# First mixing reordered on three engines, gate products cut into 64x64 halves

## The reference

```
u = rmsnorm(h, g_pre_mix)
q, k, v, xr, yr = split(u @ w_in)                    # 512, 128, 128, 512, 512 columns
s = q k^T / 8 within a window of 128; p = exp(s - m) / (sum(exp(s - m)) + exp(sink - m))
attn = p @ v                                          # 8 heads of 64, two blocks of queries
xr = causal_conv(xr, 4 taps) + conv_b
gate_r, gate_i = xr @ w_a, xr @ w_x                   # 8 diagonal blocks of 64x64 each
r, i = sigmoid(gate_r + b_a), sigmoid(gate_i + b_x)
a = exp(-8 r softplus(-lam)); hr = scan(a, sqrt(1 - a^2) * (i * xr))
rec = gelu(yr) * hr
h = h + rmsnorm(concat(attn, rec) @ w_out, g_post_mix)
```

## Time and profile before

| | us |
|---|---|
| median of 3 runs | 888.44 |
| lowest, highest | 888.41, 888.63 |
| the profiled execution | 888.37 |
| its span | 886.6 |
| PE busy in the span | 874.9 |
| DVE busy | 585.6 |
| ACT busy | 525.3 |
| POOL busy | 24.6 |

### The profile page before, as it was taken

One profiled execution on the slowest core, in us unless ns is written; L12 is line 12 of the kernel. 1 busy time (PEld: TensorE's weight loads), 2 busy tenths in 40 slices (PEclk: granted clock), 3 DMA queues, 4 the chain that ended last, 5 costly groups with the idle time before them and its releaser, 6 DMA issues.

```text
span 886.6 us, 17878 instructions
## 1 busy us (share of the span) xinstructions
PE 874.9 (99%) x7067; PEld 811.9 (92%) x7067; DVE 585.6 (66%) x950; ACT 525.3 (59%) x927; POOL 24.6 (3%) x36
## 2 busy tenths in 40 slices
PE   9999999999999999999999999999999999999997
PEld 6988899999998999999999999999988999999986
DVE  4689865555556666668787878556767555554576
ACT  6478664444446765665968676765558444444463
POOL 4100300000000000000000000000000000000000
PEclk9999999999999999999999999999999999999999
DMA  9913775555554464545324142335565565565541
GB/s 282 271 65 112 199 199 190 188 188 188 189 189 143 143 190 143 161 151 163 125 67 144 50 143 77 116 122 170 185 201 191 190 189 189 189 189 189 183 150 48
DMA packets 107655, 143.24 MB, mean 162 GB/s; under 512 B 3032, under 2 KB 95448, under 8 KB 107600
## 3 DMA queue, kind: packets, MB, share of 16 engines
q1 hardware_dynamic: 105648, 137.60, 48.4%
q0 software_dynamic: 1744, 4.67, 2.4%
q10 hardware_dynamic: 208, 0.20, 0.1%
HBM read 141.41 MB, written 1.05 MB: 161 GB/s over the span
## 4 chain that ended last, share of the span: by engine, by line
PE 90%; DVE 5%; ACT 4%; issue 1%; DMA 0%; DVEq 0%; ACTq 0%
PE ps L1853 17%; PE ps L1855 16%; PE ps L1854 16%; PE ps L1859 9%; PE ps L1861 9%; PE ps L1860 9%; PE ps L2237 2%; PE ps L2224 1%; PE ps L2245 1%; ACT wh L640 1%; PE ps L1951 1%; PE ps L2212 1%; DVE wl L1214 1%; DVE R L1250 0%; PE ps L1932 0%
## 5 line engine op out<-in xcount | busy, mean ns | idle before, releaser
L1214 DVE TENSOR_TENSOR wl<-w_raw,wh 128x1024 fp32r<-128x1024 f32 x251 | 304.7, 1223 | 216.2 <-ACT wh L640 215.6
L1853 PE MATMUL ps<-xTh,wh 128*128 128x256 f32 (+1 forms) x1160 | 331.2, 286 | 1.3 <-DVE xTl L1240 0.8
L1855 PE MATMUL ps<-xTh,wl 128*128 128x256 f32 (+1 forms) x1160 | 326.3, 281 | 0.0
L1854 PE MATMUL ps<-xTl,wh 128*128 128x256 f32 (+1 forms) x1160 | 326.3, 281 | 0.0
L640 ACT ACTIVATE wh<-w_raw 128x1024 fp32r<-128x1024 f32 x251 | 263.6, 1055 | 80.0 <-PE ps L1861 58.9
L1853 PEld LDWEIGHTS ps<-xTh,wh 128*128 128x128 f32 x1160 | 219.0, 189 | 5.3 <-issue 3.2
L1854 PEld LDWEIGHTS ps<-xTl,wh 128*128 128x128 f32 x1160 | 218.3, 188 | 1.9 <-issue 1.0
L1855 PEld LDWEIGHTS ps<-xTh,wl 128*128 128x128 f32 x1160 | 219.3, 189 | 0.0
L1859 PE MATMUL ps<-wh,y 128*128 128x512 f32 x224 | 87.9, 392 | 0.0
L1861 PE MATMUL ps<-wh,y 128*128 128x512 f32 x224 | 87.6, 391 | 0.0
L1860 PE MATMUL ps<-wl,y 128*128 128x512 f32 x224 | 87.1, 389 | 0.0
(11 more groups left out here) (390 smaller groups left out, 1265.3 us busy)
## 6 DMA issues: line engine op xcount, KB each, us to landing
w_raw<-in_w_in_dram SPq DMA_DIRECT2D x42, 1024.0 KB, 5.2
w_raw<-in_w_ff_dram SPq DMA_DIRECT2D x32, 1024.0 KB, 5.3
w_raw<-in_w_ffn_gate_dram SPq DMA_DIRECT2D x11, 1024.0 KB, 5.4
w_raw<-in_w_ffn_up_dram SPq DMA_DIRECT2D x11, 1024.0 KB, 5.3
w_raw<-in_w_ffn_down_dram SPq DMA_DIRECT2D x11, 1024.0 KB, 5.0
w_raw<-in_w_out_dram SPq DMA_DIRECT2D x8, 1024.0 KB, 4.9
w_raw<-in_w_proj_a_dram SPq DMA_DIRECT2D x4, 1024.0 KB, 5.4
w_raw<-in_w_proj_b_dram SPq DMA_DIRECT2D x4, 1024.0 KB, 5.3
```

What stands on the lines that cost most here:

```text
L1214: TT(low_part, raw_unit(SLOT[p], j, layout), high_part.bitcast(F32), ALU.subtract).then_inc(w_lo, 1)
L1853: mm(out, wh_, xh, start=first, stop=False)
L1854: mm(out, wh_, xl, start=False, stop=False)
L1855: return mm(out, wl_, xh, start=False, stop=last)
```

## The change

Four edits, all in the first mixing.

1. On DVE, `soft_sums(1)` goes ahead of `lo(13)`, `lo(14)` ahead of the combination that frees the square root, the scans ahead of what were `lo(16)` and `lo(17)`; these two low parts leave DVE.
2. They go to GpSimd, as one `tensor_tensor` each, which waits for the high part and for all low parts in front of it. DVE's `lo(18)` waits for both.
3. On PE, two weight steps of `rec_unit(0)` go ahead of `scores(0)`, one of `rec_unit(2)` ahead of `scores(1)`, three of `gelu_unit(1)` ahead of `p_transposes(0)`.
4. Each gate product of 128x128 becomes two of 64x64, one for each diagonal block, on the upper and the lower half of the partitions.

```
@@ gpsimd
             pool.dma_start(cst[:, C_COS:C_END], A["cst"][:, C_COS:C_END]).then_inc(cst_loaded, 16)
 
+            for n in (16, 17):
+                pool.wait_ge(w_hi, n + 1)
+                pool.wait_ge(w_lo, n)
+                high_part, low_part = unit_parts(n, "rows")
+                pool.tensor_tensor(low_part, raw_unit(SLOT[n // 2], n % 2, "rows"), high_part.bitcast(F32), ALU.subtract).then_inc(w_lo, 1)
+
             pool.wait_ge(gain_used, 1)
@@ vector
             convolve(1)
             lo(12)
+            soft_sums(1)
             lo(13)
-            soft_sums(1)
 
             dve.wait_ge(i_act, LT)
...
             link(TT(a2, a_, a_, ALU.mult))
+            lo(14)
             dve.wait_ge(a_tanh_out, 2 * LT)
             STT(th_, a2, 1.0, th_, ALU.add, ALU.mult).then_inc(m2_out, 1)
             oT_lo(0)
-            lo(14)
             lo(15)
             dve.wait_ge(mult_out, 1)
             link(TT(xc, a2, xc, ALU.mult))
             oT_lo(1)
-            lo(16)
             for m in range(LT):
                 ins = dve.tensor_tensor_scan(r_g[:, m, :], a_[:, m, :], xc[:, m, :], 0.0, ALU.mult, ALU.add)
             link(ins)
-            lo(17)
             dve.wait_ge(gelu_out, 1)
             TT(gy, gy, r_g[:, :, META:T1], ALU.mult).then_inc(rec_out, 1)
+            dve.wait_ge(w_lo, 18)
             lo(18)
@@ tensor
+            def some(steps, n):
+                for _ in range(n):
+                    next(steps)
+
+            steps = rec_unit(0)
+            some(steps, 2)
             for b in range(2):
                 pe.wait_ge(emptied[b], EMPTIED[6][b])
             scores(0)
-            rec_unit(0)
-            rec_unit(1)
+            run(steps)
+            run(rec_unit(1))
+            steps = rec_unit(2)
+            some(steps, 1)
             scores(1)
-            rec_unit(2)
-            rec_unit(3)
-            gelu_unit(0)
+            run(steps)
+            run(rec_unit(3))
+            run(gelu_unit(0))
+            steps = gelu_unit(1)
+            some(steps, 3)
             p_transposes(0)
-            gelu_unit(1)
+            run(steps)
...
-                mm(fm[:, m % 2, 0:T1], wa_bd[:, m, :], xc[:, m, :], start=True, stop=True)
-                mm(acc[:, m, 0:T1], wx_bd[:, m, :], xc[:, m, :], start=True, stop=True).then_inc(r_ps, 1)
+                for bd, out in ((wa_bd, fm[:, m % 2, 0:T1]), (wx_bd, acc[:, m, 0:T1])):
+                    for half in (slice(0, 64), slice(64, P)):
+                        last = mm(out[half], bd[half, m, half], xc[half, m, :], start=True, stop=True)
+                last.then_inc(r_ps, 1)
```

More of the change, by code:

```diff
@@ L2047, in rec_unit @@
             def rec_unit(m):
-                run(fm_steps(6 + m, xTh, xTl, 0, T1))
+                return fm_steps(6 + m, xTh, xTl, 0, T1)
             def gelu_unit(m):
-                run(fm_steps(10 + m, xTh, xTl, META, S))
+                return fm_steps(10 + m, xTh, xTl, META, S)
+            def some(steps, n):
[3 more added lines that the diff above has]
+            some(steps, 2)
             for b in range(2):
@@ L2070, in _ @@
                 pe.wait_ge(emptied[m % 2], EMPTIED[GATE_UNIT][m % 2] - LT // 2 + m // 2)
-                mm(fm[:, m % 2, 0:T1], wa_bd[:, m, :], xc[:, m, :], start=True, stop=True)
-                mm(acc[:, m, 0:T1], wx_bd[:, m, :], xc[:, m, :], start=True, stop=True).then_inc(r_ps, 1)
+                for bd, out in ((wa_bd, fm[:, m % 2, 0:T1]), (wx_bd, acc[:, m, 0:T1])):
+                    for half in (slice(0, 64), slice(64, P)):
+                        last = mm(out[half], bd[half, m, half], xc[half, m, :], start=True, stop=True)
+                last.then_inc(r_ps, 1)
             p_transposes(1)
[L2074 to L2077, removed]
+            run(gelu_unit(2))
+            steps = gelu_unit(3)
+            some(steps, 2)
             outputs(1)
```

## The result

The changed kernel takes 890.25 us (median of 20 runs, 888.69 to 890.66), the kernel before, timed beside it, 888.74 (20 runs, 888.22 to 889.31). The ratio is 1.0017, its 95% interval 1.0011 to 1.0023: slower by 1.0 to 2.0 us, and the time lies above the forecast range, which ended at 889.4.

The account below looks back on a forecast made before the run. PE was taken as the bound, busy 874.9 of 886.6 us, with 1.76 us of waits as ceiling; 888.37 - 0.63 - 0.25 + 1.08 + 0 gave 888.57, with 0.07 for the median 888.6; range 887.2 to 889.4.

Parts of the forecast that it names:

- Weight steps: On PE: steps ahead of the scores bring later ones 0.63 us earlier; three ahead of the first transposes delay these 0.26.
- The two steps ahead of `scores(0)`: On PE: six products run inside the 0.72 us wait, so all weight steps behind the scores come 0.63 us earlier.
- DVE's chain to the second transposes: From DVE's copy to the softmax sums, ending at 68.10: PE starts the second transposes at 68.20, gaining 0.88 us.
- Gate halves: Gate products on PE: the two 64x64 halves run side by side, 0 us.
- POOL: Low parts on GpSimd: 2.35 us each; lo(16) holds DVE's root product until 79.45, +1.08 us.
- The step from no hindrance to the held product: At the output projection's second tokens: the delayed root product adds 1.08 us, PE starting at 81.52 instead of 80.44.
- No hindrance: Rival, DVE's root product beside POOL: hindered for less than the 0.4 us margin, 887.6, up to 887.9; chance 0.33.
- DVE first: Rival, DVE's root product beside POOL: DVE always goes first, POOL works in its pauses, 888.9 us; chance 0.10.
- Serial gates: Rival, gate products on PE: halves run one after the other, +2.5 us, 890.9; chance 0.05.
- The case of all waits gone: Rival, PE in the first mixing: all three waits vanish, -1.76 us, 886.7; chance 0.03.
- the middle case: The forecast, DVE's root product: the later instruction waits for the earlier, PE's second tokens 0.20 us later, 888.6; chance 0.45.
- something not thought of: Anywhere: a remainder for causes the prediction did not list, no size given; chance 0.04.

Follow-up runs that it names:

- a4: The kernel before with the gate halves alone, no other edit: 888.34 us, ratio 1.0002 to the kernel before.
- a2: The changed kernel with the low parts of units 16 and 17 back on DVE, nothing on POOL: 888.98 us, ratio 1.0005 to the kernel before.
- b1: The kernel before with only the low parts of units 16 and 17 moved from DVE to GpSimd: 889.72 us, ratio 1.0014.
- m2: The changed kernel without the three gelu_unit(1) steps ahead, low parts back on DVE, plus idle GpSimd fills: 887.87 us, ratio 0.9993 to the kernel before.
- a1: The changed kernel with the three weight steps of gelu_unit(1) back behind the first transposes: 888.67 us, ratio 1.0004 to the kernel before.
- m1: The changed kernel without the three gelu_unit(1) steps ahead, low parts back on DVE, plus idle two-input GpSimd products: 891.26 us, ratio 1.0031.
- g3: The changed kernel with lo(11) moved ahead of soft_sums(0) on DVE, GpSimd's low parts kept: 889.02 us, ratio 1.0007 to the kernel before.

## Why the prediction was wrong

**Weight steps: the step that failed.** "The three steps ahead of the first transposes (nine products, 1.1 us) move these from ... 56.56 to about 57.65, that is 0.26 later than before." The nine products were taken as ready to run. They need `lo(11)`, which DVE's list has behind the first softmax product: before, that product runs from 55.89 to 57.25, and the low part behind it until 57.17 + 1.22 = 58.39. The timeline of DVE before:

```profile
57.17 1.22 DVE L1214 TENSOR_TENSOR wl<-w_raw,wh 128x1024 fp32r<-128x1024 f32 x1
```

At their old place, from 59.06, the products found it done. In the changed kernel PE therefore stood 1.25 us in front of them, and the first transposes came 1.63 late, not 0.26. The softmax that they were to cover had long ended: in the changed kernel it was done at 57.06, PE could start at 58.25. Everything needed was in the trace of before; what the moved products wait for at their new place was not asked. The two steps ahead of `scores(0)` did what was said (PE at 56.72 is 0.62 ahead, 0.63 forecast).

**DVE's chain to the second transposes** was right in its links: the copy of the transposed block started 2.01 us later than before on the clock, 1.63 counted from the last query product, one low part (1.13) is saved, and 0.50 is left. Forecast with the 0.26, it was -0.88. The difference of 1.38 is the error at the first transposes, nothing else. The idle time left there, 1.04, is the 1.0 of the forecast.

**Gate halves**: 0, right; a4 shows it alone.

**POOL**: right in kind and size. Shifted by 0.38 for the later start and by 1.38 for the failed step, the forecast has POOL's piece from 78.83 (79.00 in the trace), the product's end at 82.52 (82.56) and the second tokens at 83.28 (83.34). The step from no hindrance to the held product was put at 1.08; the changed kernel against a2 shows 1.11. (The prediction calls 7.21 the only DVE row beside a POOL product; one at 8.32, of the same line, length and kind, lies beside it too, and changes nothing.) That POOL's `lo(17)` goes ahead of the scans happened too, and they take 4.04 instead of 2.56; `rec_lo` at 89.63 + 1.23 ends ahead of PE's need here, but not in b1. The Trainium skill, "SBUF — State Buffer", section "Who interferes with whom", is borne out by these runs: the one issued later stands until the earlier one is over (1.78 us at 79.63), whichever was issued first goes first (b1), and a GpSimd instruction that only writes holds nothing up (m2).

**Rivals.** No hindrance and DVE first fall with the rows at 79.63 and 79.00. Serial gates fall with a4. The case of all waits gone falls with the 1.04 us left ahead of the second transposes. What happened is the middle case with a wait that had a place only in the 0.04 left for something not thought of: 888.6 + 1.38 = 890.0 against 890.25. The rest of 0.27 is about what the kernel before differed by itself, 888.74 beside the change against the 888.44 that the prediction started from.

## What to carry to other kernels

When work is moved ahead of a wait to fill it, list for each moved instruction what it waits for itself, and find in the other engines' lists where that is made: filling a wait of 0.15 us with products whose operand comes 1.2 us later costs more than the wait. Low parts or other two-tensor work given to GpSimd aren't free because GpSimd is idle: look at which VectorE instructions with two SBUF tensors can start inside them, and who waits behind those. A gain on one engine's list is real only as far as the next one in the chain; here a high part ahead of ACT's root held 0.5 us of it.

## What the runs showed of the hardware

VectorE's product of two SBUF tensors of 1088 columns takes 1.28 us alone, and 2.61 to 2.93 when issued inside a GpSimd product of two SBUF tensors; in the changed kernel, a1, m1 and g3 it ends 1.14 to 1.15 us behind GpSimd's end, whether it had stood for 1.46 or for 1.79 us until then, so but for some 0.13 us it doesn't advance meanwhile. GpSimd's piece of 1024 columns takes 2.41 when nothing holds it and 3.1 to 3.3 when issued inside VectorE's product. `oT_lo(1)` with one tensor in PSUM took its 0.69 beside a GpSimd piece, and a fill 0.95 beside the product's 1.29. A diagonal pair of 64x64 fp32 products of 272 columns takes no longer than one 128x128 product: eight pairs 3.88 us.
